# Head sums of an RWKV stage: one block-diagonal product each, or four 64x64 products

## The reference, cut to what matters

```python
kk = kk / jnp.maximum(jnp.sqrt(jnp.sum(kk * kk, axis=-1, keepdims=True)), 1e-12)
...
var = jnp.mean(jnp.square(y - mu), axis=-1, keepdims=True)
yn = (y - mu) * lax.rsqrt(var + GN_EPS) * gn_g + gn_b
bonus = jnp.sum(rh * kh * r_k, axis=-1, keepdims=True) * vh
```

## Time and profile before

| what | value |
|---|---|
| median of 3 runs | 1075.15 us (1074.27 to 1075.35) |
| the profiled execution | 1076.2 us, span 1074.2 us |
| PE busy | 977.5 us (91%), 6604 instructions |
| DVE busy | 474.2 us (44%), 1053 instructions |
| ACT busy | 289.5 us (27%), 474 instructions |
| POOL busy | 226.8 us (21%), 336 instructions |
| mean granted TensorE clock | 0.990 |

### The profile page before, as it was taken

How to read it: one execution, slowest core, us unless ns; L and a number is a source line. 1 busy time by engine, 2 the same in 40 slices (tenths; PEclk the granted TensorE clock), 3 DMA queues, 4 the chain that set the end, 5 groups by cost and what they waited for, 6 DMA issues and landing times.

```text
span 1074.2 us, 17631 instructions
## 1 busy us (share of the span) xinstructions
PE 977.5 (91%) x6604; PEld 432.9 (40%) x6605; DVE 474.2 (44%) x1053; ACT 289.5 (27%) x474; POOL 226.8 (21%) x336
## 2 busy tenths in 40 slices
PE   7999999999999999799998888888888888887774
PEld 3644455455455446344444333333333333322221
DVE  0696453564463364422328333444434444443333
ACT  1114322322322133100014233333333333322322
POOL 2000010010010010023124233333333333332322
PEclk9999999999999999999999999999999999999998
DMA  9432311221220220472946999999999999999992
GB/s 286 122 79 59 79 41 42 64 55 41 59 59 24 59 59 3 162 275 117 396 172 220 377 412 416 391 417 416 415 416 414 416 415 415 415 414 417 416 400 103
DMA packets 96900, 256.68 MB, mean 239 GB/s; under 512 B 17484, under 2 KB 62540, under 8 KB 72016
## 3 DMA queue, kind: packets, MB, share of 16 engines
q1 hardware_dynamic: 85024, 240.57, 58.8%
q0 software_dynamic: 11024, 13.20, 3.7%
q10 hardware_dynamic: 800, 2.15, 0.5%
HBM read 260.66 MB, written 21.23 MB: 262 GB/s over the span
## 4 chain that ended last, share of the span: by engine, by line
PE 52%; DMA 17%; issue 9%; DVE 7%; SPq 7%; POOL 5%; ACT 2%; POOLq 1%; ACTq 0%; DVEq 0%
PE proj L1464 12%; DMA y_rows<-const,raw 12%; PE proj L1423 11%; SPq L506 7%; PE bank L1640 5%; PE proj L1651 5%; PE bank L1566 4%; PE bank L1780 3%; DMA xT_sb<-w_gu 3%; DMA pass_sb<-x_rows,raw 2%; POOL pass_sb L578 2%; POOL const L595 2%; PE proj L1431 1%; PE bank L1801 1%; PE proj L1442 1%
## 5 line engine op out<-in xcount | busy, mean ns | idle before, releaser
L1464 PE MATMUL proj<-xT_sb,ring 128*128 128x512 f32 x384 | 185.7, 611 | 0.0
L1780 PE MATMUL bank<-arena 128*64 128x512 f32 x544 | 122.8, 596 | 19.5 <-DMA arena<-w_gu 10.7
L1423 PE MATMUL proj<-xT_sb,ring 128*128 128x512 f32 (+1 forms) x272 | 119.1, 594 | 0.0
L1347 DVE TENSOR_TENSOR const<-bank,const 128x512 f32<-128x512 f32 x33 | 22.8, 691 | 161.2 <-DMA const<-y_rows,raw 161.2
L1464 PEld LDWEIGHTS proj<-xT_sb,ring 128*128 128x128 f32 x384 | 66.9, 189 | 63.0 <-issue 59.2
L1780 PEld LDWEIGHTS bank<-arena 128*64 128x64 f32 x544 | 42.3, 136 | 99.8 <-issue 81.2
L1423 PEld LDWEIGHTS proj<-xT_sb,ring 128*128 128x128 f32 (+1 forms) x272 | 50.8, 188 | 64.6 <-issue 64.5
L852 ACT ACTIVATE pass_sb<-bank 128x256 f32<-128x256 f32 x33 | 12.7, 384 | 199.2 <-PE bank L1780 199.2
L1780 PE MATMUL bank<-gates,arena 128*64 128x512 f32 x256 | 57.4, 596 | 7.9 <-PE bank L1801 4.1
L1640 PE MATMUL bank<-branches,arena 128*128 128x512 f32 x128 | 58.0, 615 | 6.3 <-DVE branches L1106 6.3
L595 POOL DMA_INDIRECT const<-y_rows,raw x33 | 34.7, 1052 | 124.8 <-DMA y_rows<-const,raw 124.0
(11 more groups left out here) (310 smaller groups left out, 1334.8 us busy)
## 6 DMA issues: line engine op xcount, KB each, us to landing
arena<-w_gu SPq DMA_DIRECT2D x64, 1024.0 KB, 25.1
gates<-w_gu SPq DMA_DIRECT2D x32, 1024.0 KB, 23.6
arena<-w_down SPq DMA_DIRECT2D x24, 1024.0 KB, 26.7
ring<-w_in SPq DMA_DIRECT2D x42, 512.0 KB, 3.9
gates<-w_down SPq DMA_DIRECT2D x16, 1024.0 KB, 25.5
xT_sb<-w_gu SPq DMA_DIRECT2D x16, 1024.0 KB, 27.0
branches<-w_down SPq DMA_DIRECT2D x16, 1024.0 KB, 27.4
ring<-w_gu SPq DMA_DIRECT2D x16, 1024.0 KB, 25.9
```

What stands on the lines that cost most here:

```text
L1423: ins = pe.matmul(proj[0:w, b, :], ring[:, slot, k, 0:w], xT_sb[:, k, :], start=(k == 0), stop=(k == KT - 1))
L1464: ins = pe.matmul(proj[:, gate_at["bank"], :], ring[:, gate_at["slot"], k, :], xT_sb[:, k, :], start=(k == 0), stop=(k == KT - 1))
L1780: ins = pe.matmul(bank[SLOTS * h:SLOTS * h + SLOTS, 0, :], xeT[:, k % 4, SLOTS * (k // 4):SLOTS * (k // 4) + SLOTS], gu[k // 2][:, k % 2, ...
```

## The change

The three sums become four 64x64 products each, `ones` of 64x64 with one head and one half of the tokens. The first half of the tokens goes to the head's own partitions, the second half to the other head's, so that the four use all four quadrants of the array; head h writes bank b + h. The bonus sum moves from bank 3 to banks 4 and 5, the y sum from bank 1 to banks 0 and 1, the kk sum from bank 2 to banks 2 and 3. The instruction that reads a sum becomes four, each for one head and one half of the tokens, and brings the second half back to the head's own partitions. Waits and semaphores stay; the last of the four gives the signal.

```diff
+        def head_halves(b):
+
+            for h in range(2):
+                for half, to in ((slice(0, T // 2), KS[h]), (slice(T // 2, T), KS[1 - h])):
+                    yield h, half, bank[to, b + h, half]
...
-                act.activation(norm, bank[:, 2, :], ACT.Sqrt).then_inc(s_norm, 1)
+                for h, half, sums in head_halves(2):
+                    ins = act.activation(norm[KS[h], half], sums, ACT.Sqrt)
+                ins.then_inc(s_norm, 1)
...
-                act.activation(yrs, bank[:, 1, :], ACT.Sqrt, bias=par_col(EPS_GN)).then_inc(s_yroot, 1)
+                for h, half, sums in head_halves(0):
+                    ins = act.activation(yrs[KS[h], half], sums, ACT.Sqrt, bias=par_sb[KS[h], EPS_GN:EPS_GN + 1])
+                ins.then_inc(s_yroot, 1)
...
-                dve.tensor_tensor(bonus, bank[:, 3, :], v_, MUL).then_inc(s_ch, 1)
+                for h, half, sums in head_halves(4):
+                    ins = dve.tensor_tensor(bonus[KS[h], half], v_[KS[h], half], sums, MUL)
+                ins.then_inc(s_ch, 1)
...
+            def head_sums(b, src):
+
+                halves = list(head_halves(b))
+                for n in (0, 2, 1, 3):
+                    h, half, to = halves[n]
+                    ins = pe.matmul(to, C("ones")[KS[h], 0:HD], src[KS[h], half], start=True, stop=True)
+                return ins
...
-                pe.matmul(bank[:, 2, :], C("head_ones"), sq, start=True, stop=True).then_inc(s_ss, 1)
+                head_sums(2, sq).then_inc(s_ss, 1)
                 pe.wait_ge(s_pr, hp + 1)
-                pe.matmul(bank[:, 3, :], C("head_ones"), kkn, start=True, stop=True).then_inc(s_bs, 1)
+                head_sums(4, kkn).then_inc(s_bs, 1)
...
-                pe.matmul(bank[:, 1, :], C("head_ones"), ysq, start=True, stop=True).then_inc(s_var, 1)
+                head_sums(0, ysq).then_inc(s_var, 1)
```

## The result

The changed kernel takes 1091.26 us (median of 4 runs, 1090.67 to 1092.34) against 1075.25 for the kernel before (4 runs, 1074.27 to 1076.98): 16.0 us slower, ratio 1.0148 with a 95% interval of 1.0131 to 1.0166. The direction was as forecast, the amount was not: 11.9 us were forecast, and the measured time lies 0.26 us above the upper end of the range. The profiled execution took 1090.67 us, its span is 1089.0.

The account below looks back on a forecast made before the run. It took the ScalarE and VectorE chain at each pair's head as the bound: heads 7.8, tail 1.22, y sums -0.15, giving 8.9, plus clock 3.0, made 11.9 us and a median of 1087.0; range 1080.0 to 1091.0.

Parts of the forecast that it names:

- What bounds the heads: Head of each pair: tile copy, table load, square root, VectorE chain, transpositions set the time; TensorE already waits 0.42 us.
- The sums on TensorE: Four-part sums: lone sum 0.84 for 0.86 us; two together end filling 0.45 earlier, worth nothing; y sums save 0.15 in all.
- The quarter reads: Four reads end to end: square root +0.95, bonus product +1.00 per head, y root +1.22 us showing only in pair 3.
- The low ends: Smaller growth if reads overlap: square root +0.62, bonus product +0.72, y root +0.89 us.
- first sum of 8.9: Whole kernel before any clock loss: heads 7.8, plus tail 1.22, minus 0.15 saved by y sums, in us.
- The clock: Behind TensorE's 2.8 us stops at pair heads: two of four bring half clock, 1.5 us each, 3.0 together.
- rival of four falls: All four head stops bring half clock at 1.65 us each: 8.9 + 6.6 = 15.5, 1090.7 us; chance 0.10.
- Overlapping quarters: Reads on ScalarE and VectorE run 0.28 and 0.33 apart, stop 2.2, clock stays up: 1081.3 us; chance 0.20.
- No fall: Clock stays at 1.00 behind the head stops, so 8.9 us alone: 1084.0 us; chance 0.25.
- TensorE setting the pace: At the heads, TensorE's saving on sums comes through and quarter reads are covered: 1073.1 us; faster had chance 0.04.
- taken up inside the pair: Head's delay is absorbed because something else releases later steps; only the tail's 1.22 shows: 1076.4 us; chance 0.04.

Follow-up runs that it names:

- early table: Changed kernel with the square root's table loaded ahead of the copy of the last projection tile: 1081.02 us, ratio 1.0047.
- stop alone: Kernel before, sums and reads untouched, with four more VectorE products of 128x512 ahead of the bonus in each pair: 1092.46 us, ratio 1.0148.
- own partitions: Changed kernel with the second half of the tokens also at the head's own partitions, so four products on two quadrants: 1088.92 us, ratio 1.0118.
- unused products: Changed kernel with three more TensorE products, results read by nobody, between a pair's gate filling and its transpositions: 1085.43 us, ratio 1.0084.
- kk sum alone: Kernel before with only the kk sum and its square root changed, the bonus sum one product in bank 4: 1080.12 us, ratio 1.0045.
- bonus sum alone: Kernel before with only the bonus sum and its product changed: 1082.09 us, ratio 1.0062.

## Why the prediction was right in kind and short in amount

**What bounds the heads: right.** The chain of tile copy, table load, root, VectorE, transposition was read correctly from the kernel before. The early table is the proof: it moved the transposition by 1.35 us in the changed kernel with the sums as they were.

**The sums on TensorE: right.** The step gave 0.84 for a lone sum and took 0.05 as saving; measured 0.07 per pair. For two together it gave 0.45 by which the filling ends earlier; the stop of 2.89 is 0.42 + 1.97 + 0.50, so it measured 0.50. Worth nothing there, as said.

**The quarter reads: right.** Predicted 1.55, 1.68 and 1.91 us, measured 1.55, 1.71 and 1.91. Per head 1.95 predicted, 1.97 measured; the tail 1.22 and 1.22. The low ends (0.62 and 0.72 for the first two) would have needed reads that do not move between halves of the partitions. So the first sum of 8.9 stands: 7.88 - 0.21 + 1.22 = 8.89.

**The clock: the step that failed.** "I take it that two of the four stops bring a fall like the one at 647 ... 1.5 each, 3.0 together." There were three falls, and they cost 2.90, 1.67 and 1.50 between transposition and scores, 6.07 together. The mechanism was right and its term was mis-sized by a factor of two: three falls for two, at 2.02 us each on average for 1.5, the long one in pair 0 alone 2.90. The bound on the price, 1.65, came from one row of 3.3 us at half clock. The row next to it there shows 5.2 us at half clock with TensorE busy all through behind the 6.26 us stop; that would have given 2.6 for the upper price and some 10 us for four falls, and a range that reaches past 1091.26. The prediction passed over it. In the run with the stop alone all four heads had falls, 7.5 us together; with the changed kernel that is seven of eight heads behind stops of 2.8 to 2.9 us. So three or four falls were likelier than two, and the 1.65 at the range's upper end was too low. That the rival of four falls (1090.7) comes within 0.6 us of the measured time is in part luck: a fall too many made up for a price too low, 6.6 against 6.07.

The small remainder, 16.0 - 8.9 - 6.1 = 1.0 us, has no single place. The two profiled executions differ by 14.5, with +0.5 in the scores stage and 0.77 - 1.51 = -0.7 at start and end; the one before lies 0.95 above its median, the one after 0.59 below. Of the 4.3 us by which the forecast was short, 3.1 are the clock's; with these alone the median would have been some 1090.2, inside the range.

**The rivals.** Overlapping quarters fell on the 1.55 and 1.71; that rival also took a stop of 2.2 us to be free of falls, and stops of 1.59 had three in the run with own partitions. No fall is what the changed kernel with unused products shows: 1085.43, against 1084.0 predicted for it. TensorE setting the pace fell on the stop of 2.89; it came true only after the chain had been shortened. The delay was not taken up inside the pair: every stretch from the scores on is as long as before, within 0.4 us.

## What to carry to other kernels

Ask of a faster product who waits for its end: here a table load that has nothing to do with the sum ended later, and the instructions that read the sum paid for its new shape in each of the four pairs. A layout that spreads a result over partitions so that the products run side by side makes its readers run end to end, on ScalarE and on VectorE, whenever the partitions move (here by 0.2 us for four reads with three moves against one). And count a new stop of TensorE twice, once for its length and once for the half-speed work behind it; the second was as large as three quarters of the first here.

## What the runs showed of the hardware that was not expected

The clock fell behind shorter stops than the prediction reckoned with (the shortest with a fall in its rows was 2.45 us), and not by length alone. Heads in the profiled executions, with TensorE at work without a break before and the transpositions behind each stop:

| stop, us | kernel | heads with the clock at 0.50 behind the stop |
|---|---|---|
| 0.31 | changed, unused products | 0 of 4 |
| 0.42 | before | 0 of 4 |
| 1.44 | kk sum alone | 0 of 4 |
| 1.51 | bonus sum alone | 0 of 4 |
| 1.54 | changed, early table | 1 of 4 |
| 1.59 | own partitions | 3 of 4 |
| 2.82 | stop alone | 4 of 4 |
| 2.89 | changed | 3 of 4 |

A head with the same instructions and the same stop may or may not have one; what decides it the runs do not show. Nor does the fall have to come within the stop: with own partitions the first transposition of pair 1 starts at 230.38, TensorE is busy without a break from there at a granted clock of 1.00, and only at 231.9 does the clock fall to 0.50. The rows behind two of the falls in that run, columns as in the stages above, show TensorE busy throughout at half speed:

```profile
231.90:235.30 3.40, 3.40 (x17) 3.40 (x17) 0.73 (x2) 1.11 (x3) 2.33 (x3) 0.50 0.00 0
...
409.40:412.80 3.40, 3.40 (x15) 2.88 (x14) 1.38 (x2) 0.70 (x2) 2.00 (x2) 0.50 0.00 0
```

The other thing is on ScalarE: that an instruction whose partitions move waits for the one before it to end holds there as on VectorE, 1.55 for four roots with three moves and 1.31 with one.
